# Gates' inputs ahead of the pages and prompt keys, and the sample's pages on two queues, in a hybrid decoder step

## The reference, cut to what matters

```
proj = rmsnorm(x) @ w_in                         # q, k, v, index queries and keys, u
idx  = top_256(relu(qi . ki) weighted by wi)     # causal, per query token
a_o  = softmax attention of q over the chosen k, v (8 heads, 2 key/value heads of 64)
y    = S5 state-space scan of u;  z = gelu(y)
s_o  = z * sigmoid(z @ w_glu + b_glu)            # the gates: (tokens x 512) @ (512 x 512)
x    = x + rmsnorm(concat(a_o, s_o) @ w_out)
out  = x + rmsnorm(square(relu(rmsnorm(x) @ w_up)) @ w_down)
```

## Time and profile before

| | |
|---|---|
| median of 3 runs | 3682.56 us (3680.38 to 3683.88) |
| the profiled execution | 3676.49 us, its span 3674.8 us |
| busy share of the span | PE 83%, PEld 65%, DVE 50%, ACT 45%, POOL 34% |
| chain that ended last | PE 49%, DVE 12%, issue 10%, ACT 5%, POOL 3%, DMA 3% |
| mean TensorE clock granted | 0.912 of full speed |

### The profile page before, as it was taken

How to read it: one execution, slowest core, us unless ns; L and a number is a source line. 1 busy time by engine, 2 the same in 40 slices (tenths; PEclk the granted TensorE clock), 3 DMA queues, 4 the chain that set the end, 5 groups by cost and what they waited for, 6 DMA issues and landing times.

```text
span 3674.8 us, 47108 instructions
## 1 busy us (share of the span) xinstructions
PE 3039.5 (83%) x15352; PEld 2401.7 (65%) x15352; DVE 1842.5 (50%) x4116; ACT 1637.8 (45%) x2873; POOL 1244.2 (34%) x1149
## 2 busy tenths in 40 slices
PE   7998544647778889996799999968999999699996
PEld 5886421314556668764577886646778888588885
DVE  4432962762357984367685332666772333511112
ACT  3332412522546755575563446745634444322222
POOL 1332620313013561253264114522672112224444
PEclk9999766868879999998899999889999999899998
DMA  4444344546336564354454223343543213544443
GB/s 152 138 140 151 86 128 131 136 133 205 102 130 216 207 248 134 116 200 146 164 182 166 82 79 122 128 171 120 184 165 114 70 61 129 188 146 152 174 154 111
DMA packets 219182, 529.45 MB, mean 144 GB/s; under 512 B 57514, under 2 KB 114924, under 8 KB 192924
## 3 DMA queue, kind: packets, MB, share of 16 engines
q1 hardware_dynamic: 199900, 499.65, 39.6%
q0 software_dynamic: 9824, 18.40, 1.6%
q10 hardware_dynamic: 9216, 8.39, 0.7%
HBM read 399.43 MB, written 134.12 MB: 145 GB/s over the span
## 4 chain that ended last, share of the span: by engine, by line
PE 49%; DVE 12%; issue 10%; ACT 5%; POOL 3%; DMA 3%; SPq 1%; ACTq 1%; POOLq 0%; DVEq 0%
PE r L1620 16%; PE r L1652 12%; PE po L1700 4%; PE tr L1691 3%; ACT junk_a_b L1969 2%; POOL acc_b L2104 1%; PE sc L1668 1%; PE sc L1679 1%; PE sc L1678 1%; PE r L1809 1%; DVE junk_v_b L2343 1%; DVE trial_b L2295 1%; PE tr L1668 1%; PE r L1765 1%; POOL hr_b L2085 1%
## 5 line engine op out<-in xcount | busy, mean ns | idle before, releaser
L2104 POOL TENSOR_TENSOR acc_b<-acc_b,part_b 128x512 f32<-128x512 f32 x375 | 516.1, 1396 | 495.8 <-ACT part_b L1920 494.9
L1652 PE MATMUL r<-ready_b,h_b 128*128 128x512 f32 x2304 | 569.4, 403 | 42.2 <-ACT part_b L1920 38.2
L1652 PEld LDWEIGHTS r<-ready_b,h_b 128*128 128x128 f32 x2304 | 437.4, 193 | 159.2 <-ACT part_b L1920 50.7
L1620 PE MATMUL r<-x_hi_b,ready_b 128*128 128x512 f32 x1536 | 493.6, 395 | 5.4 <-DVE x_lo_b L2209 2.8
L2085 POOL TENSOR_TENSOR hr_b<-hr_b 128x512 f32<-128x512 f32 x128 | 148.4, 1159 | 777.1 <-ACT hr_b L1907 776.8
L1969 ACT ACTIVATE junk_a_b<-score_b,trial_b 128x384 int8<-128x384 f32 (+13 forms) x266 | 347.5, 1306 | 103.5 <-DVE trial_b L2295 102.4
L1620 PEld LDWEIGHTS r<-x_hi_b,ready_b 128*128 128x128 f32 x1536 | 290.8, 189 | 75.8 <-issue 10.1
L1920 ACT ACTIVATE part_b<-r 128x512 f32<-128x512 f32 x390 | 223.5, 594 | 217.1 <-PE r L1652 130.8
L1700 PEld LDWEIGHTS po<-V_sb,pT_b 128*128 128x128 f32 x2176 | 287.5, 192 | 23.1 <-issue 3.1
L1620 PE MATMUL r<-x_lo_b,ready_b 128*128 128x512 f32 x768 | 301.0, 392 | 0.0
L1996 ACT ACTIVATE pT_b<-tr 128x512 f32<-128x512 f32 (+3 forms) x320 | 168.8, 527 | 264.4 <-PE tr L1691 262.6
(11 more groups left out here) (407 smaller groups left out, 6028.6 us busy)
## 6 DMA issues: line engine op xcount, KB each, us to landing
ready_b<-ws_u SPq DMA_DIRECT2D x96, 1024.0 KB, 6.7
ready_b<-ws_d SPq DMA_DIRECT2D x96, 1024.0 KB, 5.0
ws_u<-up_b SPq DMA_DIRECT2D x32, 1024.0 KB, 8.8
ws_d<-dn_b SPq DMA_DIRECT2D x30, 1024.0 KB, 6.5
raw_b<-w_out SPq DMA_DIRECT2D x64, 256.0 KB, 3.2
raw_b<-w_up SPq DMA_DIRECT2D x32, 512.0 KB, 5.5
raw_b<-w_down SPq DMA_DIRECT2D x32, 512.0 KB, 4.1
kv_b<-kv_pages SPq DMA_DIRECT2D x96, 128.0 KB, 3.8
```

The lines of the kernel that those rows point to most:

```text
L1620: mm = pe.matmul(x[:], wt[:, c], y[:, k], start=k == n == 0, stop=(k, n) == (KD - 1, 2))
L1652: mm = pe.matmul(x[:], f[:, tok], w[:, col], start=c == n == 0, stop=(c, n) == (KQ - 1, 2))
L2104: pool.tensor_tensor(dst, dst, part[:, add_no[key] % 2, :], ALU.add).then_inc(add_pool, 1)
```

## The change

SP's order at `SF` 0 becomes: `w_glu`, bias, block 0 of `zb`, its pages of chunk 0, block 1 of `zb`, prompt keys and values. It now waits there for `wt_full` and for `rl_ok` before the first of them. The pages are issued by SP and POOL alone: SP all four of the first sequence, POOL all four of the second. Each reads its four page numbers by one load into four registers. ACT issues none and calls `sample_loads` no more. PE waits for four pages in each of the slot's two semaphores, where it waited for five and three.

```
-        by_queue = {"sp": [(0, p) for p in range(PPC - 1)], "pool": [(1, p) for p in range(PPC - 1)], "act": [(b, PPC - 1) for b in range(2)]}
-        fetched = [len(by_queue["sp"]) + len(by_queue["act"]), len(by_queue["pool"])]
+        by_queue = {"sp": (0, mybir.EngineType.SP), "pool": (1, mybir.EngineType.Pool)}
 
         def load_pages(eng, i, queue):
             r, c = divmod(i, NC)
-            for b, p in by_queue[queue]:
-                n = (2 * r + b) * NPAGE + c * PPC + p
-                page = eng.value_load(spt[0:1, n:n + 1], min_val=0, max_val=A["kv_pages"].shape[0] - 1)
-                eng.dma_start(kv[:, i % SLOTS, b, p], A["kv_pages"][bass.ds(page, 1)].rearrange("o p k c -> (o p) k c")
-                              ).then_inc(kv_ld[queue == "pool"][i % SLOTS], 16)
+            b, which = by_queue[queue]
+            n = (2 * r + b) * NPAGE + c * PPC
+            _, pages = nc.values_load_multi_w_load_instructions(spt[0:1, n:n + PPC], engines=(which,), min_val=0, max_val=A["kv_pages"].shape[0] - 1)
+            for p in range(PPC):
+                eng.dma_start(kv[:, i % SLOTS, b, p], A["kv_pages"][bass.ds(pages[p], 1)].rearrange("o p k c -> (o p) k c")
+                              ).then_inc(kv_ld[b][i % SLOTS], 16)
...
-                        sample_loads(sp, "sp", u)
                         if u == ("SF", 0):
-                            load_keys()
+                            sp.wait_ge(wt_full, NC + 1)
                             sp.wait_ge(rl_ok, 2 * NC + 2)
                             sp.dma_start(wglu[:], A["w_glu"]).then_inc(gl_ld, 16)
                             sp.dma_start(bglu[:], A["b_glu"]).then_inc(gl_ld, 16)
                             load_outputs(0)
+                        sample_loads(sp, "sp", u)
+                        if u == ("SF", 0):
                             load_outputs(1)
+                            load_keys()
...
-                            pe.wait_ge(kv_ld[b][i % SLOTS], 16 * fetched[b] * (i // SLOTS + 1))
+                            pe.wait_ge(kv_ld[b][i % SLOTS], 16 * PPC * (i // SLOTS + 1))
...
-                        sample_loads(act, "act", u)
```

## The result

| | before | changed kernel |
|---|---|---|
| median of the first runs (4 and 4) | 3681.47 us (3679.53 to 3683.88) | 3656.78 us (3654.04 to 3665.12) |
| ratio, 95% interval | | 0.9936 [0.9919, 0.9954] |
| profiled execution, span | 3674.8 us | 3652.4 us (3654.04 us in all) |
| the same kernels measured once more (21 and 5 runs) | 3678.32 us (3671.68 to 3685.53) | 3661.52 us (3660.43 to 3667.74) |
| ratio, 95% interval | | 0.9955 [0.9942, 0.9969] |

The direction was right, the size too small. The two measurements of the same kernel differ by 5 us in their medians, and the second median lies inside the range.

What follows compares the result with a forecast made beforehand. The wait for `zb` was taken to delay gates and search, with page issue, ACT's copies and queries limiting the passes. 16.4 + 0.9 - 5.4 = 11.9 us gained gave 3664.6 profiled, 3670.7 us as median; range 3659 to 3680.

Steps and rivals of the forecast that it cites:

- The gates' inputs: Before the first gate: PE's wait for block 0 of `zb` ends at 630.5 instead of 646.88, 16.4 us earlier.
- The cover of block 2: At the gates: block 2 of `zb` arrives in time, cost nothing; if not, up to 3 us lost.
- ACT's issues in the search: In the search on DVE: twelve page issues taken off ACT gain 0.9 us (0 to 1.5).
- The pages in the passes: Attention passes 0 to 2: later pages and queries lose 0.9, 1.6 and 2.9 us, together -5.4 us.
- ACT's relief: `SV` units and `SO`: two pages per unit off ACT would save some 4 us a pass, limited by late pages.
- The load of four: Page issue on POOL and SP: four registers load in 0.55 us, bounds 0.29 to 1.16; chunks take 4.0 and 3.7 us.
- the slack: Pages land before PE uses them by 2.6 us in pass 0 to 1 and 1.9 in pass 1 to 2, capping gains.
- The sign that PE would wait for pages: In the `SS` units of passes 1 and 2 PE would wait for pages, which it did not before.
- rival 1: Page loads: further registers cost nearly what the first does, passes lose up to 19.3 us, about 3684; chance 0.24.
- Rival 2: Passes: ACT's relief comes out in full, gain 25 us, 3657; chance 0.10.
- Rival 3: SP's queue backs up under half of all pages, three passes lose 28 us more, 3699; chance 0.06.
- rival 4: Gates: their wait is not the limit or the order does not shorten it, passes lose 5, 3687; chance 0.04.

Runs made afterwards that it cites:

- e1_order: Kernel before with only SP's new order at `SF` 0, pages still on three engines with single loads: 3665.57 us, ratio 0.9961.
- e4_nocheck: Changed kernel without the bounds check of the page numbers: 3649.14 us, ratio 0.9921.
- e3_single: Changed kernel with four register loads of one number each instead of one load of four: 3676.99 us, ratio 0.9998.
- e12_pool_later: e8_defer with POOL's pages of chunk 0 issued four gates later, at `SF` 3: 3644.11 us, ratio 0.9902.
- e8_defer: e4_nocheck with SP's pages of the last three chunks of pass 2 issued behind the second query tile's queries: 3637.38 us, ratio 0.9890.

## Why the prediction was wrong

**The gates' inputs: right.** The wait for `zb` is 16.1 us shorter, against 16.4, and ended at 631.71, which is 630.8 on the clock of the kernel before, against 630.5. The cover of block 2 held: the same 144 matmuls take 58.82 us, 59.22 before. (They are 16 whole gates and two short ones, so a whole gate takes more than the 3.3 us of the forecast; nothing came of it.) e1_order gives the same by itself.

**ACT's issues in the search: 0.9 forecast, 0.4 measured**, 16.5 at the end of the search less 16.1 at the gates. So small a term can't be told from chance: from the first gate to pass 0 the changed kernel took 129.7 us, before 130.05, but e4_nocheck, with the same relief, 131.0.

**The pages in the passes: the sum near, by luck.** Forecast were -0.9, -1.6 and -2.9, together -5.4 us; measured is 12.0 - 16.5 = -4.5. The forecast set its three terms at three places: the last scores of pass 1, `SS` (1, 7), those of pass 2, `SS` (2, 7), and the first scores behind the queries. The local gain there is 831.37 - 814.12 + 0.95 = 18.2, 873.31 - 857.44 + 0.95 = 16.8 and 913.41 - 902.77 + 0.95 = 11.6 us. After 16.5 at pass 0 these are steps of +1.7, -1.4 and -5.2; 0.4 came back behind.

The sizes first. ACT's relief is 4.9 us in pass 0 (776.93 to 819.36 before, 761.40 to 798.96 now), not 4. The load of four costs 0.33 us, not 0.55: it lies at the lower bound, and chunks take 3.65 and 3.32 us instead of 4.0 and 3.7. With these the forecast's own terms would be 2.6 - 1.05 = +1.6, 1.9 - 1.05 = +0.9 and -0.4, in all +2. The first is borne out: PE waits for pages 1.98 + 2.05 us in pass 1 and keeps what the slack allows. (It waits 1.15 + 3.11 in pass 2. Two of the four have "issue" for a releaser, but stand ahead of a chunk's scores, where the earlier trace rows have no wait. The sign that PE would wait for pages came true.) The other two terms miss 7 us, and the load that was taken too long covers most of that by chance.

The rows show where most of the 7 us arose. The matmuls right behind the second wait of a pass take 1.98 and 1.97 us, where those of the earlier trace rows take 1.08; the granted clock of pass 1 was 0.78 (798.96 to 841.14), before 0.82. SP's pages of pass 2 start at 871.42, 884.77 - 871.42 + 0.95 = 14.3 us earlier than before, 2.5 less than PE's lead of 16.8. Their issue costs 0.4 more: they end at 894.73, 12.94 + 0.95 = 13.9 us earlier than at 907.67. From there to PE's start the queries take 8.04 us, 5.74 before, another 2.3. PE had come at 902.77 - 14.46 = 888.31 us, 23.2 us earlier by the common clock than at 910.56 before, so its wait grew from 2.85 to 14.46 us, not to 8: the stream of pages and queries set the time of this stretch, not PE. Why the queries take 2.3 us longer on their way was not looked into.

**The load of four, rule and measurement.** The Trainium skill, "Runtime: NRT & Kernel Launch", section "Instruction fetch mechanics", gives about 200 ns per register even in bulk. The estimate of 0.8 us that follows from it is not borne out, and rival 1 falls with it: one load of four took 328 ns in the median on POOL. e3_single shows that single loads would have put the change at no gain, so the choice between the bounds was the right one to worry about. Two slips in the working changed nothing: a load of 1.16 us makes a chunk on POOL 4.60 us and the passes -18.1, not -19.3, and at 0.8 us the gain would be 6.7, not 6.

**What failed is the sum itself: it left out the end of the program.** The forecast said that whatever shortens the wait moves all behind it forward and that the program ends on one chain. So it put a change of the 9.4 us behind POOL's last addition at nothing, without a reason. That POOL's queue gets 32 more DMAs was followed through the passes, and not to the block's end. The page change shortens that tail by 5.5 us in all ten profiled executions in which POOL issues 128 pages, so local gain and tail make 9.9 + 5.5 = 15.4 us in the second execution, where the medians of the second measurement differ by 16.8; in the first execution 12.0 + 5.5 - 0.95 + 5.9 of drift make its 22.4. With the tail the forecast would have been 3665.2 us. That the first median fell out of the range took the drift as well, which is chance: less either of the two it lies inside, as the second median, 3661.52, does.

**The baseline.** The forecast started from the median of three runs, 3682.56; the median of 21 is 3678.32. From there with 11.9 us of gain it would have said 3666.4, and with the tail 3660.9, against 3661.52 measured. The single medians of the changed kernel, 3656.78 and 3661.52, are themselves 5 us apart. Rival 2 gave 3657, but ACT's relief did not come out in full: 4.9 us in pass 0 had become 1.7 at `SS` (1, 7). That its number is near is no support for it. Rival 3's queue did not back up (SP's 28 issues at 0.83 us each), and rival 4 is excluded by e1_order.

## What to carry to other kernels

When an engine needs a stream of transfers piece by piece, what it gains by the relief of another engine is handed back at the next place where the stream is late. So find the queue that sets the pace and shorten its chunk (joint register loads, no bounds check: 3.50 us for three pages became 2.69 for four), and put what another stage needs ahead of pages that nobody wants yet. That last step, the order of one queue, was worth 12 us or more, where the page change alone was worth nothing that could be measured. And read the last microseconds of a span as a stage of its own: who reaches the block's end last, and what did the change do to that engine's queue?

## What the runs showed of the hardware

- The end of a block waits for POOL's closing `DRAIN`, and its length depends on the DMAs that POOL issued more than 2700 us earlier: 3.9 to 10.8 us from its last arithmetic instruction to the end, of which SP's last store hides 3.2.
- One register load of four consecutive numbers takes 328 ns on POOL and 298 on SP, a load of one 289 and 270.
- The bounds check of a page number holds a register instruction of 0.15 us, and without the four checks a chunk is 0.96 us shorter on POOL, 0.36 more than these four instructions take.
- The granted clock moves these numbers too: the same matmuls kept PE busy 212.9 us in e12_pool_later and 207.7 in e8_defer, at 0.81 against 0.86 and 0.85 in passes 0 and 1.
- The same program drifts by several us between two executions in parts that no experiment touches: the changed kernel's gain grew by 5.3 us between 965 and 3630 us in one and by 0.7 in the other.
